# Down product of the ConvFFN as one level of Strassen's identity over four row tiles, in place of three passes over the weights

## The reference

```python
f = (jax.nn.gelu(conv) * (x @ W['w_ffn_gate'])) @ W['w_ffn_down']
x = layer_norm(ALPHA * x + f, W['ln2_g'], W['ln2_b'])
x = x + jax.nn.sigmoid(x @ W['w_ple_gate']) * (p_emb @ W['w_ple'])
```

## Time and profile before

| | us |
|---|---|
| median of three runs (2485.43 to 2488.14) | 2486.68 |
| the profiled execution itself | 2487.03 |
| its span, first to last instruction | 2485.2 |
| PE busy | 2422.2 (97%) |
| DVE / ACT / POOL busy | 1125.6 / 532.0 / 735.3 |
| mean granted TensorE clock, of full speed | 0.995 |

### The profile page before, as it was taken

How to read it: one execution, slowest core, us unless ns; L and a number is a source line. 1 busy time by engine, 2 the same in 40 slices (tenths; PEclk the granted TensorE clock), 3 DMA queues, 4 the chain that set the end, 5 groups by cost and what they waited for, 6 DMA issues and landing times.

```text
span 2485.2 us, 30784 instructions
## 1 busy us (share of the span) xinstructions
PE 2422.2 (97%) x11127; PEld 1561.0 (63%) x11127; DVE 1125.6 (45%) x2969; ACT 532.0 (21%) x1312; POOL 735.3 (30%) x819
## 2 busy tenths in 40 slices
PE   8999999999999999999999999999999999999999
PEld 4544665555556776788884478888888854443443
DVE  4875726776763444424225863334333310506312
ACT  0001025666653333111111221011111100101100
POOL 0000014554543001666543534233342310202100
PEclk9999999999999999999999999999999999999999
DMA  5424630021039786422225101111111153223300
GB/s 183 102 85 100 247 129 1 1 90 47 1 95 249 239 233 202 146 77 85 85 76 158 53 31 52 35 52 35 35 52 35 52 179 104 102 102 131 125 30 34
DMA packets 176447, 240.25 MB, mean 97 GB/s; under 512 B 52379, under 2 KB 127777, under 8 KB 174761
## 3 DMA queue, kind: packets, MB, share of 16 engines
q1 hardware_dynamic: 170282, 214.53, 27.5%
q0 software_dynamic: 4848, 14.19, 1.7%
q10 hardware_dynamic: 1168, 9.58, 1.2%
HBM read 216.18 MB, written 37.99 MB: 102 GB/s over the span
## 4 chain that ended last, share of the span: by engine, by line
PE 58%; DVE 2%; ACT 0%; issue 0%; DVEq 0%
PE ps L2166 35%; PE ps L2294 12%; PE ps L2323 6%; PE ps L2219 4%; PE ps L2298 1%; DVE xT L153 1%; PE ps L2326 0%; ACT xT L2343 0%; DVE xT L1335 0%; DVE arena L1337 0%; DVE arena L1326 0%; DVE arena L1328 0%; PE ps L2159 0%; DVE queries L1337 0%; DVE queries L1328 0%
## 5 line engine op out<-in xcount | busy, mean ns | idle before, releaser
L2166 PE MATMUL ps<-xT,arena 128*128 128x272 f32 x1920 | 474.7, 394 | 6.2 <-ACT arena L2396 5.3
L2166 PEld LDWEIGHTS ps<-xT,arena 128*128 128x128 f32 x1920 | 364.9, 191 | 82.7 <-ACT arena L2396 5.8
L2166 PE MATMUL ps<-queries,arena 128*128 128x272 f32 x1312 | 332.6, 393 | 1.8 <-DVE arena L1337 1.0
L2294 PE MATMUL ps<-arena 128*128 128x512 f32 x704 | 305.0, 594 | 0.7 <-DVE arena L2617 0.7
L2166 PEld LDWEIGHTS ps<-queries,arena 128*128 128x128 f32 x1312 | 250.0, 191 | 54.2 <-DVE arena L1337 1.5
L2294 PEld LDWEIGHTS ps<-arena 128*128 128x128 f32 x704 | 132.9, 190 | 172.1 <-issue 171.2
L236 PE MATMUL ps<-arena,xT 128*128 128x512 f32 (+1 forms) x512 | 198.2, 550 | 2.1 <-DMA arena<-in_w_in 1.3
L943 ACT ACTIVATE arena<-arena 128x640 f32<-128x640 f32 (+15 forms) x256 | 164.7, 644 | 68.8 <-DVE arena L899 48.7
L1008 POOL TENSOR_SCALAR arena<-arena,gates 128x55 f32<-128x55 f32 (+15 forms) x192 | 122.8, 649 | 176.7 <-DVE arena L907 176.5
L236 PEld LDWEIGHTS ps<-arena,xT 128*128 128x128 f32 x512 | 97.7, 191 | 102.2 <-issue 93.2
L798 PE MATMUL ps<-ident,arena 128*128 128x128 f32 (+4 forms) x880 | 138.0, 284 | 11.0 <-POOL arena L1008 5.2
(11 more groups left out here) (301 smaller groups left out, 3033.9 us busy)
## 6 DMA issues: line engine op xcount, KB each, us to landing
arena<-in_w_ffn_down SPq DMA_DIRECT2D x66, 512.0 KB, 3.2
arena<-in_cache_fox_kv SPq DMA_DIRECT2D x72, 256.0 KB, 4.5
arena<-in_w_in SPq DMA_DIRECT2D x16, 1024.0 KB, 5.2
xT<-in_cache_fox_kv SPq DMA_DIRECT2D x56, 256.0 KB, 6.1
arena<-in_cache_nsa_kv SPq DMA_DIRECT2D x64, 192.0 KB, 7.4
arena<-in_w_ffn_up SPq DMA_DIRECT2D x11, 1024.0 KB, 5.3
arena<-in_w_ffn_gate SPq DMA_DIRECT2D x11, 1024.0 KB
bias_rows<-rev_dram ACTq DMA_DIRECT2D x8, 1160.0 KB
```

What stands on the lines that cost most here:

```text
L2166: mm = pe.matmul(ps[:, first + BANK_OF[z], 0:PIECE], weight[:, j, :], moving[:, j, :], start=(j == 0 and z in (1, 6, 5, 7)), stop=(j == kk ...
L2294: mm = pe.matmul(ps[:, q + h, :], hT[:, c, t0:t0 + m], at.w_down[load % RING][:, cols], start=(c == 0), stop=(c == NFF - 1))
```

## The change

The down product becomes Strassen's identity (Winograd's form, seven products in place of eight) over the whole product at once. Rows 0 to 511 and 512 to 1023 are the two halves of the rows; even and odd chunks, paired as j = 0 to 10 (`NJ` = 11), are the halves of the sum; columns 0 to 511 and 512 to 1023 are the halves of the output. Each product runs over 11 pairs and four tiles of 128 rows, in one set of four PSUM banks: products in the order 1, 6, 2, 5, 3, 7, 4, of which 1, 2, 7 and 4 use banks 0 to 3 and 6, 5 and 3 use banks 4 to 7. Products 2, 3 and 4 add onto the banks of 1, 5 and 7. Products 7 and 4 also carry the sample tile's matmuls, two per pair j, into banks 5 and 4.

- Sums of h: POOL makes S3, S1 and S2 (33 instructions of 128x512) and S4 (11), in place in `hT` except S3.
- Sums of weights: DVE makes `t2` (22), `t1` (11), `t3` (11) and `t4` (22), all 128x512 with both inputs in SBUF.
- Weights come in pieces of 128x512 (256 KB): 88 through a ring of 16 slots (`STREAM`, `down_piece`), 44 straight into `hT` (`late_pieces`), in SP's queue, which now also loads the x1 rows, nine transfers, between products 6 and 2's pieces.
- Banks are read by ACT (product 1, four copies) and DVE (`both_kept`, `c11_read`, `p5_read`, `c12_read`, `p7_read`, `c21_read`), and `rows_set2` adds kept values to the rows.
- Tiles 0 to 3 are normalised and turned on DVE between `c12_read` and the first seven `t4`; tiles 4 to 8 between the PLE units' DVE work. PE's transposes of tiles 6 to 8 and ACT's `save` are gone. PLE units use banks 6, 0 and 2 (and the one after each).
- PE starts product 1 without waiting for the last up/gate step's combination; buffers move; one more group of semaphores is cleared by POOL at the start of `trunk` (`k.retire(over)`).

```diff
-OUT_GROUP = 3
 TILES = [(i * P, min(P, R - i * P)) for i in range(NT)]
 LAST = NT - 1
-PASSES = [list(range(s, min(s + OUT_GROUP, NT))) for s in range(0, NT, OUT_GROUP)]
-RING = 5
-LOADS = [(n, c) for n in range(len(PASSES)) for c in range(NFF)]
+NJ = NFF // 2
+DOWN = (1, 6, 2, 5, 3, 7, 4)
+STREAM = ([(1, j, "B11") for j in range(NJ)] + [(6, j, b) for j in range(NJ) for b in ("B12", "B11", "B22")] +
+          [(2, j, "B21") for j in range(NJ)] + [(5, j, b) for j in range(NJ) for b in ("B12", "B11")] + [(3, j, "B22") for j in range(NJ)])
+RING = 16
...
+def down_steps(z, j):
+    return sum(NJ + 4 if y in (7, 4) else NJ + 3 for y in DOWN[:DOWN.index(z)]) + (j + 1 if j < NJ - 1 else NJ + 4 if z in (7, 4) else NJ + 3)
+
+def down_banks(z, i):
+    return down_steps(z, NJ - 2) + i + 1
+
...
+        self.ring = ([at(25088 + 512 * e, 512) for e in range(4)] + [flat[:, c, 0:512] for c in range(KD)] +
+                     [flat[:, c, 512:1024] for c in range(4, KD)])
+        self.partial = [flat[:, i, 512:1024] for i in range(4)]
+        self.s3 = at(27136, NJ, 512)
...
+        k.retire(over)
...
+            def released(z, j, b):
+                if z == 6 and b != "B22":
+                    sp.wait_ge(t_made, j + 1)
+                elif z == 5 and b == "B11":
+                    sp.wait_ge(t_made, NJ + j + 1)
+                else:
+                    sp.wait_ge(d_step, down_steps(z, j))
+            def down_piece(m):
+                z, j, b = STREAM[m]
+                if m >= RING:
+                    released(*STREAM[m - RING])
+                sp.dma_start(at.ring[m % RING], down_source(io, j, b)).then_inc(d_there[m % RING], 16)
+            def late_pieces(j, low, high):
+                for b, cols in ((low, slice(0, 512)), (high, slice(512, 1024))):
+                    sp.dma_start(at.hT[:, 2 * j, cols], down_source(io, j, b)).then_inc(late_in[j], 16)
...
+            for m in range(4, RING):
+                down_piece(m)
+            sp.wait_ge(h_done, NFF)
+            sp.wait_ge(tail_out, 32 * NPAIRS_F)
+            for m in range(RING, STREAM.index((2, 0, "B21"))):
+                down_piece(m)
+            for i, (t0, m) in enumerate(TILES):
+                sp.dma_start(at.rows2[i][0:m, :], io["x1_rows"][t0:t0 + m, :]).then_inc(x1_there[i], 16)
+            first_late = STREAM.index((3, 0, "B22"))
+            for m in range(STREAM.index((2, 0, "B21")), first_late):
+                down_piece(m)
+            for j in range(NJ):
+                down_piece(first_late + j)
+                sp.wait_ge(s4_summed, j + 1)
+                sp.wait_ge(d_step, down_steps(5, j))
+                late_pieces(j, "B22", "B12")
+            for j in range(NJ):
+                sp.wait_ge(d_step, down_steps(7, j))
+                late_pieces(j, "B21", "B11")
...
+            def down_operands(z, j):
+                even, odd = at.hT[:, 2 * j, :], at.hT[:, 2 * j + 1, :]
+                a11, a21, a12, a22 = even[:, 0:512], even[:, 512:T], odd[:, 0:512], odd[:, 512:T]
+                left = {1: a11, 6: a11, 2: a12, 3: a12, 5: a21, 7: at.s3[:, j, :], 4: a22}[z]
+                if z in (7, 4):
+                    return left, a12
+                b = {1: "B11", 6: "B22", 2: "B21", 5: "B12", 3: "B22"}[z]
+                return left, at.ring[down_slot(z, j, b)[0]]
...
+            def operands_there(z, j):
+                if z == 1:
+                    pe.wait_ge(h_done, 2 * j + 1)
+                if z == 6:
+                    pe.wait_ge(h_summed, 3 * j + 3)
+                if z == 3:
+                    pe.wait_ge(s4_summed, j + 1)
+                if z in (1, 2, 3):
+                    slot, count = down_slot(z, j, {1: "B11", 2: "B21", 3: "B22"}[z])
+                    pe.wait_ge(d_there[slot], count)
+                else:
+                    pe.wait_ge(t_made, NJ * (6, 5, 7, 4).index(z) + j + 1)
+            def bank_free(z, i):
...
+                if z == 2:
+                    pe.wait_ge(first_kept, i + 1)
+                if z == 5:
+                    pe.wait_ge(both_kept, i + 1)
+                if z == 3:
+                    pe.wait_ge(p5_read, i + 1)
+                if z == 7:
+                    pe.wait_ge(c11_read, i + 1)
+                if z == 4:
+                    pe.wait_ge(p7_read, i + 1)
+            def sample_rows(z, j):
+                if j == 0:
+                    pe.wait_ge(c12_read, 2)
+                pe.wait_ge(late_in[j], 32 if z == 7 else 64)
+                for odd, cols in ((0, slice(512, T)), (1, slice(0, 512))):
+                    mm = pe.matmul(ps[odd * HD:(odd + 1) * HD, 5 if z == 7 else 4, :], at.hT[:, 2 * j + odd, T:R], at.hT[:, 2 * j, cols],
+                                   start=(j == 0), stop=(j == NJ - 1))
+                return mm
+            pe.wait_ge(pair_step, DVE_STEPS * (NSTEP - 1))
+            pe.wait_ge(low_saved, NSTEP - 1)
+            for z in DOWN:
+                for j in range(NJ):
+                    operands_there(z, j)
+                    left, moving = down_operands(z, j)
+                    for i in range(4):
+                        if j == 0:
+                            bank_free(z, i)
+                        mm = pe.matmul(ps[:, (0 if z in (1, 2, 7, 4) else 4) + i, :], left[:, i * P:(i + 1) * P], moving,
+                                       start=(j == 0 and z in (1, 6, 5, 7)), stop=(j == NJ - 1), skip_group_check=z in (2, 3, 4))
+                        if j == NJ - 1:
+                            mm.then_inc(d_step, 1)
+                    if z in (7, 4):
+                        mm = sample_rows(z, j)
+                    if j < NJ - 1 or z in (7, 4):
+                        mm.then_inc(d_step, 1)
...
+                if q == 0:
+                    pe.wait_ge(c12_read, 4)
+                elif q < 3:
+                    pe.wait_ge(c21_read, 2 * q)
...
-                if q < 3:
-                    turn(6 + q, at.rows2[6 + q])
...
+            for i in range(4):
+                act.wait_ge(d_step, down_banks(1, i))
+                nc.scalar.copy(at.partial[i], ps[:, i, :]).then_inc(first_kept, 1)
...
+            deviation(0, aggregated2, std_done2)
+            for i in range(4):
+                if i < 3:
+                    deviation(i + 1, aggregated2, std_done2)
+                scale(i, TILES, g2, s2, turned2, saved2)
+            deviation(4, aggregated2, std_done2)
+            for i in range(4, NT):
+                if i + 1 < NT:
+                    deviation(i + 1, aggregated2, std_done2)
+                sigmoid(i - 4)
+                scale(i, TILES, g2, s2, turned2, saved2)
+            for q in range(NT - 4, len(UNITS)):
+                sigmoid(q)
...
+            def t1(j):
+                b12, b11 = piece_there(5, j, "B12"), piece_there(5, j, "B11")
+                nc.vector.tensor_tensor(b12, b12, b11, ALU.subtract).then_inc(t_made, 1)
+            def t2(j):
+                b12, b11, b22 = (piece_there(6, j, b) for b in ("B12", "B11", "B22"))
+                nc.vector.tensor_tensor(b12, b12, b11, ALU.subtract).then_inc(t_step, 1)
+                dve.wait_ge(t_step, j + 1)
+                nc.vector.tensor_tensor(b22, b22, b12, ALU.subtract).then_inc(t_made, 1)
+            def late_operands(j):
+                return at.hT[:, 2 * j, 0:512], at.hT[:, 2 * j, 512:T], at.hT[:, 2 * j + 1, 0:512]
+            def t3(j):
+                b22, b12, t = late_operands(j)
+                dve.wait_ge(late_in[j], 32)
+                dve.wait_ge(d_step, down_steps(3, j))
+                nc.vector.tensor_tensor(t, b22, b12, ALU.subtract).then_inc(t_made, 1)
+            def t4(j):
+                b21, b11, t = late_operands(j)
+                dve.wait_ge(late_in[j], 64)
+                dve.wait_ge(d_step, down_steps(7, j))
+                nc.vector.tensor_tensor(t, b21, t, ALU.subtract).then_inc(t_step, 1)
+                dve.wait_ge(t_step, NJ + j + 1)
+                nc.vector.tensor_tensor(t, t, b11, ALU.subtract).then_inc(t_made, 1)
...
+            for j in range(NJ):
+                t2(j)
+            for i in range(4):
+                u = at.partial[i]
+                dve.wait_ge(first_kept, i + 1)
+                dve.wait_ge(d_step, down_banks(6, i))
+                nc.vector.tensor_tensor(u, u, ps[:, 4 + i, :], ALU.add).then_inc(both_kept, 1)
+            for j in range(6):
+                t1(j)
+            for i in range(4):
+                r = half_row(i, 0)
+                dve.wait_ge(x1_there[i], 16)
+                dve.wait_ge(d_step, down_banks(2, i))
+                nc.vector.scalar_tensor_tensor(out=r, in0=r, scalar=ALPHA, in1=ps[:, i, :], op0=ALU.mult, op1=ALU.add).then_inc(c11_read, 1)
+            dve.wait_ge(both_kept, 4)
+            for i in range(4):
+                r = half_row(i, 1)
+                nc.vector.scalar_tensor_tensor(out=r, in0=r, scalar=ALPHA, in1=at.partial[i], op0=ALU.mult, op1=ALU.add).then_inc(rows_set2, 1)
```

(80 more changed lines are left out.)

209 lines of the change are left out of this document (79 added, 130 removed).

## The result

The changed kernel took 2458.16 us (median of 4 runs, 2455.57 to 2458.70), the kernel before 2486.99 beside it (4 runs, 2485.43 to 2488.14): 0.9886 of the time, 95% interval 0.9873 to 0.9898, 28.8 us less. Forecast were 2461.0 and a range of 2450 to 2473.

What follows compares the result with a forecast made beforehand. The prediction took PE, busy 97% of the span, to bound the kernel. Its terms, -34.1 - 0.6 + 7.9 + 2.2 - 2.4 + 1.5 = -25.5 us, gave 2461 us, range 2450 to 2473.

Steps and rivals of the forecast that it cites:

- wait at 7 to 4: Between products 7 and 4, PE waits for DVE's late first read of product 7's banks: 7.9 us.
- clock behind it: After PE's wait between products 7 and 4, matmuls run at a lower granted clock: 2.2 us lost, bounds 0 and 4.
- PE's products: Down product: seven products with sample matmuls take PE 290.8 us instead of 324.9, 34.1 less.
- start of product 1: Before product 1, PE needs only the tails' transposes, saving 0.6 of the 0.86 us gap.
- transposes gone: PLE units: 24 transposes leave PE, 2.4 us less.
- PLE waits: PLE units: PE waits for DVE's multiplies at units 6 and 7, 1.5 us in all.
- No wait at 7-4: Rival: POOL does not hold DVE between products 7 and 4; wait 0.8 us, no clock loss, 2452 us; chance 0.18.
- A second wait: Rival: product 2's pieces held, or `t1`/`t3` late at 5-3; some 5 us plus 2.2 of clock, 2468; chance 0.26.
- My bound of 6 us: Upper bound on load cost, if x1 rows land at half rate ahead of product 2's pieces; zero was taken.
- Loads bind: Rival: 256 KB pieces in the down product come at only 129 GB/s, giving 2514 us; chance 0.04.
- Sums on POOL: POOL's 33 sums of h, sharing with DVE's `t2`, end at 61 us, before product 6's need at 72; cost zero.
- the price of clearing one more group of semaphores: POOL's clearing at the start of `trunk`: taken as zero, bounds 0 and 1.2 us.

Runs made afterwards that it cites:

- experiment 4: Changed kernel with the sample matmuls of two pairs j made together in products 7 and 4: 2455.39 us, 0.9875 of the kernel before.
- experiment 1: Changed kernel with POOL's gain and shift started only after DVE's four reads of product 7's banks: 2447.48 us, 0.9845 of the kernel before.
- Experiments 6: Changed kernel with the ring of weight pieces cut from 16 slots to 8: 2470.20 us, one run.
- 7: Changed kernel with a ring of 8 slots and the x1 rows issued behind product 2's seventh piece: 2459.92 us, one run.
- 9: Changed kernel with POOL's gain and shift and tile 3 behind product 7's reads, sample matmuls in groups of 4, 4, 2 and 1 pairs: 2446.12 us.

## Why the prediction was right, and its terms

The forecast mechanism held: PE the bound throughout, loads and sums hidden, one wait at 7 to 4 and the clock behind it. By its own steps, for the stage (the measured value of the transposes is what is left of the stage after the others):

| term | predicted us | measured us |
|---|---|---|
| PE's products | -34.1 (290.8) | -34.1 (188.8 + 50.9 + 51.1) |
| start of product 1 | -0.6 | -0.7 |
| wait at 7 to 4 | +7.9 | +6.5 |
| clock behind it | +2.2 | +2.2 |
| transposes gone | -2.4 | -2.1 |
| PLE waits | +1.5 | +0.8 |
| sum | -25.5 | -27.4 |

- **PE's products.** Product 4 is 2247.87 to 2301.15 less the 2.2 of clock. Pitch and price of a return carried over from the earlier trace rows to 0.1 us. That merging two groups gives 0.35 was already in these numbers: two single pairs at 4.63 are 9.26, a double one in the earlier trace rows is 7.07 + 1.87 = 8.94. The expectation of experiment 4 took 0.26, because it counted the dearer lone pair (0.07) once where a merge removes two.
- **The wait.** Tile 0 was turned 12.4 us after product 3's end (2190.46), 12.9 predicted; each of the next three took the 10.2 worked out, the last ending at 43.0 (43.4). The fourteen `t4` adds took 13.5 us, not 14.5: of two unshared ones the first starts 0.61 us after the one before it and only the second 0.72, which I had taken for all. So the first read began at 56.6 (57.9). The place, the cause and what takes it away are as forecast. A slip of 0.2 stands in the forecast's own sum: 58.6 less 50.9 is 7.7, not 7.9.
- **No wait at 7-4**, the first rival, is experiment 1: predicted 9.3 us below the forecast (7.1 + 2.2), measured 8.7. It was the right counterfactual and the wrong case. It kept a wait of 0.8, and none was left.
- **A second wait**, the next rival, did not come in the changed kernel. Experiments 6, 7 and 9 show it real and near: 0.97 us once with 16 slots, 8.2 with 8, by the very mechanism named, the x1 rows in front of product 2's pieces. That it stayed away in the changed kernel was a matter of 1.7 us. My bound of 6 us was for rows landing at half rate; with 8 slots issue and landing together cost more.
- **Loads bind**, the slower rival: nothing of it. Where it mattered most the changed kernel moved

```profile
2060.00:2065.00 5.00, 5.00 (x13) 2.17 (x12) 1.39 (x2) 0.00 (x0) 0.00 (x0) 1.00 1.00 371
2065.00:2070.00 5.00, 5.00 (x13) 2.28 (x12) 0.00 (x0) 0.00 (x0) 0.00 (x0) 1.00 1.03 418
```

  371 and 418 GB/s in pieces of 256 KB and x1 rows, against 140 where the rival would begin. The rule of the Trainium skill (DMA: Bandwidth & Descriptors, section Bandwidth) on transfers under 1 MiB, which would give this rival too, disagrees with these rows. The price of 2.0 us and bytes over 436 GB/s that the prediction took with it is given by that page in its section Anatomy of one DMA — SWDGE (gpsimd) path, for transfers issued by GpSimd; the loads here are SP's.
- **Sums on POOL.** Done 55.0 us after product 1's start, not 61. Eleven triples of sums at 3.97 us, their length alone, are 43.7, as priced (42 + 2). What was overrated is the sharing, 12 us in the forecast and 5.9 measured. DVE waited 30 us for weights, so only 18 of the 22 `t2` met POOL, and each cost it 0.33, not 0.55: where both run on, a triple takes 5.02 us and three `t2` instructions pass beside it. The error cost nothing: 72 was needed.
- **PLE waits.** Nearly as worked out, 0.34 and 0.50 for 0.8 and 0.7. DVE took 12.96 us a tile, 12.9 in the forecast, whose named parts add up to 12.7.

That the median (2458.16) lies 2.8 under the forecast is the stage's 1.9 and the variation ahead of it. What was only argued: the price of clearing one more group of semaphores (taken as zero) has no run of its own. The traces agree with it: POOL stood idle 4.90 us ahead of its first instruction of `trunk` before and 5.10 after, and PE waited 0.8 us there in both. Why the granted clock falls at a place in one execution and not in the next stays open.

## What to carry over

When a product is cut out of the bounding engine, list for each bank the engine that must read it before it is used again and walk that engine's queue to the read: here 6.5 + 2.2 of 37 us came back through one DVE read queued behind work that could have stood after it. Move what nobody waits for (the gain and shift, tile 3's turn, the x1 rows) behind what somebody does; it cost a few lines each and gave 8.7 and up to 10.6 us. And compare by a stage of the trace when the rest of the program varies more than the edit is worth.

## What the runs showed that was not expected

- A group of 64-row sample matmuls between main ones costs PE 0.35 us beside its records, though nothing shows as idle: 9.28 us for two single pairs, 8.93 for a double one; four are 17.51.
- The run-to-run variation of identical code ahead of the change, 8 us in the start of the tails' transposes (2000.2 to 2008.3), is almost as large as the effect of the best single edit (8.7), and most of it goes with the granted clock.
- A 256 KB piece that landed in 3.4 us by the median took 12.3, 13.0 and 14.6 behind 4.5 MB of x1 rows: in these runs what was queued in front of a piece counted for more than its size.
- The norm, with one tensor input in SBUF, is held by POOL like the adds with two (2.75 in place of 0.81), as the prediction had assumed; the 32x32 transposes are not.
- Where DVE's and POOL's adds of 128x512 follow each other without a pause, each waits only part of the other: 1.53 to 1.72 us for POOL's in place of 1.26.
